# Deeper weight buffers for eight streamed experts of a decoder trunk on one Trainium2 core

## The reference

```python
h = h + rmsnorm(hybrid_mixer(rmsnorm(h, ...), ...), mix_norm_post[i])
h = h + rmsnorm(memory_cross_attention(rmsnorm(h, ...), ...), xa_norm_post[i])
f = swiglu(hn, w_gate, w_up, w_down)                    # layer 0, dense, 1024 -> 2816 -> 1024
f = moe_swiglu(hn, router_w, w_gate, w_up, w_down)      # layer 1, top 2 of 8 experts
h = h + rmsnorm(f, ffn_norm_post[i])
```

## Time and profile before

| | us |
|---|---|
| median of 3 executions (1566.72 to 1569.93) | 1569.04 |
| the profiled execution, device time | 1561.84 |
| the profiled execution, span from first to last instruction | 1560.0 |

### The profile page before, as it was taken

One profiled execution on the slowest core, in us unless ns is written; L12 is line 12 of the kernel. 1 busy time (PEld: TensorE's weight loads), 2 busy tenths in 40 slices (PEclk: granted clock), 3 DMA queues, 4 the chain that ended last, 5 costly groups with the idle time before them and its releaser, 6 DMA issues.

```text
span 1560.0 us, 22361 instructions
## 1 busy us (share of the span) xinstructions
PE 1447.1 (93%) x9104; PEld 1275.5 (82%) x9104; DVE 1109.1 (71%) x1069; ACT 959.6 (62%) x1110; POOL 178.3 (11%) x133
## 2 busy tenths in 40 slices
PE   7999998999989999989999998898988999998986
PEld 6979988999979799879998676676766999866664
DVE  4666545444456674566766889899998876789996
ACT  5466446333354664455445788888888545478885
POOL 6200000000033000001002005050220300100400
PEclk9999999999999999989999999999999999999998
DMA  9227524555533085335666999999999766689993
GB/s 356 93 69 273 199 84 160 181 178 183 199 135 109 4 308 193 104 109 189 243 229 230 345 392 376 399 391 385 388 379 385 256 247 234 243 299 410 374 403 146
DMA packets 54418, 385.28 MB, mean 247 GB/s; under 512 B 6288, under 2 KB 6544, under 8 KB 8496
## 3 DMA queue, kind: packets, MB, share of 16 engines
q1 hardware_dynamic: 53392, 382.10, 64.8%
q10 hardware_dynamic: 432, 1.08, 0.2%
q0 software_dynamic: 496, 0.74, 0.2%
HBM read 382.85 MB, written 1.05 MB: 246 GB/s over the span
## 4 chain that ended last, share of the span: by engine, by line
PE 71%; DVE 16%; ACT 8%; issue 3%; DMA 1%; ACTq 0%; DVEq 0%; SPq 0%
PE banks L1702 12%; PE banks L1703 12%; PE banks L1704 12%; DVE w_low L1206 10%; PE banks L1700 8%; PE banks L1701 7%; PE banks L2019 7%; PE banks L2021 5%; ACT w_high L770 4%; PE banks L1963 2%; PE banks L1914 1%; PE banks L1721 1%; PE banks L1900 1%; DVE after_heads L1484 1%; ACT rows L770 1%
## 5 line engine op out<-in xcount | busy, mean ns | idle before, releaser
L1206 DVE TENSOR_TENSOR w_low<-raw,w_high 128x2048 fp32r<-128x2048 f32 x357 | 807.7, 2293 | 241.3 <-ACT w_high L770 240.9
L770 ACT ACTIVATE w_high<-raw 128x2048 fp32r<-128x2048 f32 x357 | 679.8, 1916 | 243.0 <-PE banks L2021 94.6
L1702 PE MATMUL banks<-rows,w_high 128*128 128x256 f32 x832 | 236.9, 285 | 4.9 <-DVE rows L1207 4.9
L1700 PE MATMUL banks<-w_high,rows 128*128 128x512 f32 (+1 forms) x576 | 219.7, 388 | 18.1 <-DVE w_low L1206 13.3
L1704 PE MATMUL banks<-rows,w_low 128*128 128x256 f32 x832 | 236.1, 284 | 0.0
L1703 PE MATMUL banks<-rows,w_high 128*128 128x256 f32 x832 | 236.1, 284 | 0.0
L1701 PE MATMUL banks<-w_low,rows 128*128 128x512 f32 (+1 forms) x576 | 211.6, 374 | 0.0
L2019 PE MATMUL banks<-rows,w_high 128*128 128x320 f32 x704 | 184.9, 309 | 2.1 <-DVE rows L1201 1.3
L2021 PE MATMUL banks<-rows,w_low 128*128 128x256 f32 x704 | 183.6, 278 | 0.0
L1700 PE MATMUL banks<-w_high,eT 128*128 128x512 f32 x352 | 143.7, 408 | 38.3 <-DVE w_low L1206 28.6
L1702 PEld LDWEIGHTS banks<-rows,w_high 128*128 128x128 f32 x832 | 160.3, 193 | 6.4 <-issue 5.8
(11 more groups left out here) (201 smaller groups left out, 2065.0 us busy)
## 6 DMA issues: line engine op xcount, KB each, us to landing
raw<-in_pieces_dram SPq DMA_DIRECT2D x357, 1024.0 KB, 6.9
phase<-in_mem_dram SPq DMA_DIRECT2D x2, 1024.0 KB, 6.8
cst<-in_constants_dram SPq DMA_DIRECT2D x1, 1344.0 KB, 14.7
h_res<-in_x_dram SPq DMA_DIRECT2D x2, 512.0 KB, 4.2
phase<-in_mix_norm_post_dram SPq DMA_DIRECT2D x2, 512.0 KB, 4.6
phase<-in_xa_norm_post_dram SPq DMA_DIRECT2D x2, 512.0 KB, 6.4
phase<-in_ffn_norm_post_dram SPq DMA_DIRECT2D x2, 512.0 KB, 6.5
out_dram<-h_res ACTq DMA_DIRECT2D x2, 512.0 KB, 3.0
```

Source lines behind the costliest of these rows:

```text
L770: return act.activation(out_, in_, ACT.Copy, scale=scale)
L1206: return dve.tensor_tensor(out_, in_, plain(high), ALU.subtract)
L1700: pe.matmul(dst, stay[0], move[0], start=start, stop=False, skip_group_check=True)
L1702: pe.matmul(dst, stay[0], move[0], start=start, stop=False, skip_group_check=True)
```

## The change

While the experts run there are eight places for raw pieces (two more, `raw_more`) and four for each of the halves (`high_more`, `low_more`). ACT and DVE therefore make the halves of piece c+4, not c+3, when PE is done with piece c, and one more call of `ahead` stands before the first expert. Pieces from `c_moe + 6` = 99 on use the ring of eight places, so piece c waits for `w_low` of piece c-8.

The memory for it comes from four places. The residual rows, most constants, `poolw` and `w_forget` move into the memory that is used only before the experts. The residual rows are stored to DRAM (`kept`) before piece 99 is loaded, and SP waits for that store, for the routing counts and for the last norm. They are loaded again, with the post-norm gain, into raw places that have come free at the end. The up sums of a wide expert (`sums_up`) move into the bytes of `y_sb`, and so all four parts of `share` and of `add_share` now come before the up products in a wide expert. And the DMA scratch of the program is 8192 bytes, half of its size before.

```diff
+MORE = 2
+AHEAD = SPLIT + 1
...
-        h_res = sb("h_res", [P, TT, D])
...
-        cst = sb("cst", [P, C_END])
+        cst = sb("cst", [P, C_KEPT])
...
+            early = before_experts.enter_context(nc.sbuf_tensor("early", [P, C_END - C_KEPT], F32))
+            poolw = before_experts.enter_context(nc.sbuf_tensor("poolw", [P, DEPTH, 2, P], F32))
+            w_forget = before_experts.enter_context(nc.sbuf_tensor("w_forget", [P, DEPTH, KT, HEADS], F32))
+            h_res = before_experts.enter_context(nc.sbuf_tensor("h_res", [P, TT, D], F32))
...
+        high_more = sb("high_more", [P, PIECE], F32R)
+        low_more = sb("low_more", [P, PIECE], F32R)
+        raw_more = sb("raw_more", [P, MORE, PIECE])
+        kept = nc.dram_tensor("kept", (SEQ, D), F32, kind="Internal").ap()
...
-        sums_up = view(cst, C_STRICT, WIDE // P, SEQ)
+        sums_up = view(after_heads, D, WIDE // P, SEQ)
...
+        more_split = c_moe + SPLIT
+        def split_slot(c):
+            return c % SPLIT if c < more_split else (SPLIT, *((more_split + i) % SPLIT for i in range(SPLIT)))[(c - more_split) % AHEAD]
...
+        more_from = c_moe + RAW
+        ring = list(range(RAW, RAW + MORE)) + [(more_from + i) % RAW for i in range(RAW)]
+        def slot(c):
+            return c % RAW if c < more_from else ring[(c - more_from) % len(ring)]
...
+        h_last = view(raw_at(TOTAL), 0, TT, D)
+        gpost_last = raw_at(TOTAL + 1)[:, 0:D]
...
+            def keep_h():
+                for t in range(TT):
+                    sp.wait_ge(h_ready, TT * (3 * DEPTH - 2) + TT)
+                    sp.dma_start(kept[t * P:(t + 1) * P, :], h_res[:, t, :]).then_inc(h_kept, 16)
+                sp.wait_ge(rank_full, 1)
+                sp.wait_ge(xn_ready, TT * 3 * DEPTH)
+                sp.wait_ge(h_kept, TT * 16)
 
             def load(c, r=0, n=None):
-                if c >= RAW:
+                if c == more_from:
+                    keep_h()
+                if c >= more_from + MORE:
+                    sp.wait_ge(low_ready, c - len(ring) + 1)
+                elif RAW <= c < more_from:
                     sp.wait_ge(low_ready, r * RAW + (c - RAW + 1))
...
+                if layer == DEPTH - 1:
+                    sp.wait_ge(low_ready, TOTAL + 2 - len(ring))
                 load_gpost(layer, 2)
+            for t in range(TT):
+                sp.dma_start(h_last[:, t, :], kept[t * P:(t + 1) * P, :]).then_inc(h_back, 16)
...
             def ahead(c):
-                c += SPLIT
+                c += AHEAD
                 if c < c_moe + MIXER * EXPERTS:
-                    wait_mixed(act, c - SPLIT)
-                    act.wait_ge(raw_in[c % RAW], (c // RAW + 1) * (16 * PIECE_DMAS))
-                    move(w_high[:, c % SPLIT, :], raw[:, c % RAW, :]).then_inc(high_ready, 1)
+                    if c > more_split:
+                        wait_mixed(act, c - AHEAD)
+                    wait_loaded(act, c)
+                    move(high_at(c), raw_at(c)).then_inc(high_ready, 1)
...
+                    ahead(c_moe - 1)
                     experts(act, "act", expert)
...
-                        add_share(e - 1, 0)
-                        add_share(e - 1, 1)
+                        for i in range(4):
+                            add_share(e - 1, i)
                     sums("up", 1, s, sums_up)
...
+                        dve.wait_ge(h_back, TT * 16)
+                        add_to_rows(t, gained_rows[t], inv, h_last)
...
-    nc = bacc.Bacc("TRN2", target_bir_lowering=False, num_devices=1)
+    nc = bacc.Bacc("TRN2", target_bir_lowering=False, num_devices=1, dynamic_dma_scratch_size=8192)
```

More of the change, by code:

```diff
@@ L613, in halves_of_output, with high_at, low_at, weights_of @@
             return [(dst[:, j, :], banks[:, 2 * j:2 * j + 2, :].rearrange("p a b -> p (a b)")) for j in range(2)]
+        more_split = c_moe + SPLIT
+        def split_slot(c):
+            return c % SPLIT if c < more_split else (SPLIT, *((more_split + i) % SPLIT for i in range(SPLIT)))[(c - more_split) % AHEAD]
+        def high_at(c):
+            return w_high[:, split_slot(c), :] if split_slot(c) < SPLIT else high_more[:, :]
+        def low_at(c):
+            return w_low[:, split_slot(c), :] if split_slot(c) < SPLIT else low_more[:, :]
+        def weights_of(c, *dims):
+            return view(high_at(c), 0, *dims), view(low_at(c), 0, *dims)
+        more_from = c_moe + RAW
+        ring = list(range(RAW, RAW + MORE)) + [(more_from + i) % RAW for i in range(RAW)]
+        def slot(c):
+            return c % RAW if c < more_from else ring[(c - more_from) % len(ring)]
+        def raw_at(c):
+            return raw[:, slot(c), :] if slot(c) < RAW else raw_more[:, slot(c) - RAW, :]
+        h_last = view(raw_at(TOTAL), 0, TT, D)
+        gpost_last = raw_at(TOTAL + 1)[:, 0:D]
+        def wait_loaded(eng, c, r=0):
+            loads = r + c // RAW + 1
+            if c >= more_from:
+                loads = (c - more_from) // len(ring) + 1 + len(range(slot(c), more_from, RAW) if slot(c) < RAW else ())
+            eng.wait_ge(raw_in[slot(c)], loads * (16 * PIECE_DMAS))
         counts = {}
@@ L1191, in pre, with give_gain, add_to_rows @@
                     normed(norm(layer, 2 * q), t, xn, h_res).then_inc(xn_ready, 1)
[L1193 to L1197, removed]
+            def give_gain(dst, src, at, post=gpost):
+                return dve.tensor_tensor(dst, src, post[:, at], ALU.mult)
+            def add_to_rows(t, rows, inv, h=h_res):
+                dve.scalar_tensor_tensor(out=h[:, t, :], in0=rows, scalar=inv, in1=h[:, t, :], op0=ALU.mult,
                                          op1=ALU.add).then_inc(h_ready, 1)
@@ L1212, in split @@
                 dve.wait_ge(high_ready, r * RAW + (c + 1))
-                low(w_low[:, c % SPLIT, :], raw[:, c % RAW, :], w_high[:, c % SPLIT, :]).then_inc(low_ready, 1)
+                low(low_at(c), raw_at(c), high_at(c)).then_inc(low_ready, 1)
             def take(layer, stage, i):
@@ L1974, in outputs @@
                         wait_parts(c)
-                        wt = weights(c % SPLIT, FPS, D)
+                        wt = weights_of(c, FPS, D)
                         for b in of:
@@ L2035, in wide_expert @@
                         if e and s == 0:
-                            share(e - 1, (0, 1))
+                            share(e - 1, range(4))
                         wide_columns("up", 1, s)
-                        if e and s == 0:
-                            share(e - 1, (2, 3))
                         if s:
```

54 lines of the change are left out of this document (26 added, 28 removed).

## The result

| | before | after |
|---|---|---|
| median, executions on one chip | 1567.88 us (4) | 1526.38 us (4, 1525.41 to 1527.11) |
| ratio, 95% interval | | 0.9735 (0.9719 to 0.9751) |
| profiled execution, device / span | 1561.84 / 1560.0 us | 1527.11 / 1525.2 us |

What follows compares the result with a forecast made beforehand. It took the latency of the PE, ACT and DVE loop over three places to bound the small experts. 28.7 us there plus 1 us behind wide experts, less 1 us for risks, made 29 us: 1569.04 - 29 = 1540 us, range 1527 to 1558.

Steps and rivals of the forecast that it cites:

- Size of the gain in the small experts: Small experts: nine tenths of DVE's 31.9 us of removable idle time goes, 28.7 us; forecast case's chance 0.57.
- stretches A and B: Small experts in the profile before: A from 871.3 to 1214 us, B from 1384.4 to 1541.3 us.
- all of DVE's idle time goes: Rival, small experts: all DVE idle time goes and the expert boundary packs too; 43.8 us, 1525 us; chance 0.08.
- Just able to follow: Weight loads in small experts: the stream meets a need of 395 to 403 GB/s in A; no gain of its own.
- the stream is at its end: Rival, small experts: loads get no more than 389 GB/s, so 16 us are saved, 1553 us; chance 0.2.
- Wide experts: PE has no gap there, so more stock gives 0; at worst 1.4 us in expert 5.
- store of h: Ahead of piece 99: loads issued at about 697 us, wanted at 717.7 us; cover 15 us, cost 0.
- extra `ahead`: Before expert 0: ACT's 1.9 us and DVE's 2.3 us fall into idle time, cost 0.
- tail: End of the kernel: loads of gain vector and h come in time; 0, at worst 2 us.
- Slower through late code loads: Rival, small experts: code packets come late behind the deeper queue; at 2 us each 1578 us; chance 0.08.
- the third rival: Small experts: DVE's strict order keeps PE's waits as they are; 0 to 2 us gained, 1568 us; chance 0.07.
- My signs: Small experts: `w_high` waits under 5 us, 84 to 86 us each, DVE over 95%, 400 GB/s, landing over 10 us.

Runs made afterwards that it cites:

- only_halves: The kernel after with four places for the halves but six raw places, not eight: 1527.99 us, ratio 0.9754 to the kernel before.
- only_raw: The kernel after with eight raw places but three places for the halves, not four: 1567.45 us, ratio 0.9994 to the kernel before.
- pe_extra: The kernel after with eight matmuls per small expert done twice on PE: 1526.90 us, ratio 0.9743 to the kernel before.
- dve_less: The kernel after with `w_low` made for only half the columns in two of each small expert's 33 pieces: 1518.54 us, ratio 0.9676 to before.
- light_after: The kernel after with only three quarters of the columns of each expert piece loaded from piece 101 on: 1526.86 us, ratio 0.9747 to before.
- layout_only: The kernel after with both rings at their old length, the moved memory and smaller scratch kept: 1567.19 us, ratio 0.9994 to before.
- y_on_act: The kernel after with DVE's half of the small experts' `y_sb` move given to ACT, ahead of its next rounding: 1526.38 us, ratio 0.9735 to before.
- dve_extra: The kernel after with two of the 33 subtractions of each small expert done twice on DVE: 1549.70 us, ratio 0.9901 to before.
- all_less: The kernel after with dve_less's cut, eight matmuls per small expert left out and three quarters of each load: 1515.67 us, ratio 0.9654 to before.

## Why the prediction was wrong

**The bound before: right.** The three engines' loop over three places. Its length and not its work set 89.4 us: only_halves alone ends it, only_raw does not.

**Size of the gain in the small experts: wrong, and this is the failed step.** I forecast 28.7 us for stretches A and B; they give 29.1 + 11.7 = 40.7 us. Two terms of the sum were short by 6 us each.

First, the idle time that goes. I wrote of the waits for the fold and the turn that they "come from DVE's place behind PE in the same step, and no ring length removes them", and took nine tenths of the rest. In fact 34.7 of the 43.8 us of DVE's idle time went. Fold and turn waits went from 11.9 us to 1.2 us. They were waits because DVE, short of a `w_high` to work on, arrived early at the fold. Once DVE always has work, it is late there, and PE's fold is done. The last fold matmul and the multiply of the same step of expert 2, before and then after:

```profile
986.25 0.39 PE L1955 MATMUL banks<-eT_low,fold 128*128 128x512 f32 x1
...
986.75 0.69 DVE L1484 TENSOR_TENSOR after_heads<-after_heads,banks 128x512 f32<-128x512 f32 x1 [0.39 <-PE banks L1955]
```

```profile
981.69 0.39 PE L2023 MATMUL banks<-eT_low,fold 128*128 128x512 f32 x1
...
983.92 0.68 DVE L1550 TENSOR_TENSOR after_heads<-after_heads,banks 128x512 f32<-128x512 f32 x1
```

Before, DVE stood 0.39 us until the fold was done. After, the fold is done at 982.08 us, and DVE comes 1.8 us later. The wait belonged to the same loop, and only_raw, with three places, has it back (1.5 us per expert). What stays is elsewhere: 5.4 and 3.6 us for `w_high`, mostly behind a wide expert and at the turn of two experts.

Second, DVE's busy time, which I held fixed. It fell by 6.0 us (311.36 to 308.84, 144.45 to 140.92). One part is a `w_low` less in B, since a pair more is ready when the stretch begins (86 to 85 instructions). The other is that a subtraction of 2.28 to 2.31 us takes only 2.20 us when the next one follows at once, as one step of DVE in the chain after shows:

```profile
1032.45 2.20 DVE w_low L1275
...
1037.97 2.31 DVE w_low L1275
```

**The rival "all of DVE's idle time goes",** to which I gave 0.08 (43.8 us, 1525 us), came within 1.4 us of the median. It named the right next bound, but the closeness is partly luck: 34.7 and not 43.8 us of idle time went, and a fall of DVE's busy time that it didn't have gave 6.0 us more. Its own objection, ACT and PE at 97%, did not hold: in A they are busy 91% and 95%, and pe_extra shows that PE has room for eight matmuls more.

**The stream: right as far as it went.** "Just able to follow" is what it does: 413 GB/s over A, where I had needed 395 to 403, and dve_less shows that at 421 GB/s its own bound is level with DVE's. The case "the stream is at its end" (0.2), with 389 GB/s as all that this stage gets, is refuted by the 413 to 420 GB/s that came and by light_after. That no gain comes from eight raw places, as I took it, is confirmed by only_halves. Issue to landing grew to a median of 9.7 us in a small expert (7.3 in the earlier trace rows), without effect.

**Wide experts, store of h, extra `ahead`, tail: right.** PE has no gap in expert 5 (137.00 of 137.00 us). The 1 us that I gave to the first steps behind the wide experts didn't come: A and B hold all of the 40.7 us. Piece 99 is issued at 701.35 us, lands at 706.07 and is used at 723.23; I had a cover of 15 us and it is 17. The gain vector and the rows of h are now asked for at 1489.64 and 1490.02 us, long before use, and the tail is 18.40 us. layout_only puts all of it at 0.9994.

**Slower through late code loads: not seen.** In the small experts no idle stretch of PE, DVE or ACT over 0.3 us is without a releaser. The order of DVE's program, the third rival, holds one wait of 1.0 us per expert, not the gain.

**My signs.** DVE's share (98%) and the stream (413 to 420 GB/s) came as I wrote. DVE's waits for `w_high` fell from 34.6 to 9.0 us, not under 5, for the round trip at the turn of experts and the first steps behind a wide one stay. The small expert at 82.6 us went below my 84 to 86, by the failed step. A load landed in 9.7 us, not in over 10.

**Forecast against the profiled execution.** I expected a span of 1531 us. It is 1525.2, with the mark of expert 0 5.7 us late.

## What to carry to other kernels

In a ring between engines that each run in order, a wait shown for one partner can be the same shortage as the wait for another: an engine that runs dry arrives early everywhere. So size a longer ring by the next engine's busy time per period (here 81.4 us, and a fixed 1.2 us that only the run showed), not by adding up the waits that name the ring. Then ask what the bound behind that one is: here the stream, at 82.7 us, would have taken most of any further gain. And before moving work off the bound engine, look whether it lies ahead of a wait: 0.7 us moved from such a place gave nothing, while 2.1 us taken out of the middle gave all of it.

## What the runs showed of the hardware

**The clock in front of the experts isn't the same in each execution.** The granted clock falls to half, from 2.4 to 1.2 GHz, for short stretches, and how much time they take varies. They sum to 38.0 us in the profiled execution of before and to 54.6 us in that of after. Some 10 us of each lie in the tail, none in the experts 1 to 7, and the rest, 27.3 and 44.4 us, ahead of the mark of expert 0, nearly all of it in stretches that the change doesn't touch. Two such stretches in before, in after and in y_on_act (the column after POOL is the clock):

```profile
200.00:300.00 100.00, 93.39 (x676) 88.71 (x676) 52.87 (x63) 51.71 (x88) 0.00 (x0) 0.98 0.37 134
400.00:500.00 100.00, 92.25 (x678) 87.03 (x677) 57.98 (x63) 48.39 (x67) 27.61 (x27) 0.97 0.42 148
```

```profile
200.00:300.00 100.00, 93.63 (x660) 88.91 (x660) 52.81 (x63) 50.05 (x86) 0.00 (x0) 0.95 0.36 131
400.00:500.00 100.00, 92.25 (x656) 86.62 (x656) 56.88 (x63) 45.50 (x63) 25.55 (x27) 0.95 0.43 155
```

```profile
200.00:300.00 100.00, 93.36 (x675) 88.63 (x674) 53.11 (x64) 51.33 (x88) 0.00 (x0) 0.98 0.39 134
400.00:500.00 100.00, 92.25 (x677) 86.94 (x676) 57.58 (x63) 48.42 (x67) 27.61 (x27) 0.97 0.43 148
```

The same 100 us hold 16 to 22 matmuls fewer where the clock column is lower. The mark of expert 0 goes with it: 849.04 to 849.80 us where 24 to 27 us of half clock lie ahead of it (before, y_on_act, layout_only, dve_extra), 854.05 to 855.51 us with 41 to 44 us (only_halves, after, only_raw). That pattern isn't exact: pe_extra has its mark at 853.76 us with 31 us, all_less at 856.93 us with 44 us. The 17 us more of half clock in after can cost up to 8.5 us where PE is the bound, so they can account for the 5.7 us between the two profiles. The times of one kernel lie in two heaps along the same line (layout_only: 1561.5 to 1562.5 us at a mean granted clock of 0.988 to 0.990, and 1565.6 to 1571.1 us at 0.981 to 0.987). No run set the clock, so that the dips are the cause, and why an execution gets more or fewer of them, stays open. For the reader: compare two profiles from a mark behind such a stretch, not from the start.

**A full DMA share doesn't say that transfers are late, or how much is left.** The share read 0.99 at 388 GB/s before and 1.01 at 420 GB/s after, and a quarter of the bytes less gained nothing in either. It read 1.01 at 421 GB/s in dve_less as well, where the stream did bind. Nor is a wait for a landed piece enough: only_halves has 3.5 us of such waits in a small expert and is no slower than the kernel after. The Trainium skill (DMA: Bandwidth & Descriptors, Specifications) gives about 358 GB/s for one core from HBM. The same page, in a note further down (section Bandwidth), calls this about what each of two cores gets when both of the HBM domain stream, and gives up to 425 GB/s for a core alone; I had overlooked that. This trace agrees with the note: 420 GB/s over 82 us and 413 over 314 us. The limit that did show is 421 GB/s, in dve_less.
